# Hybrid decoder trunk, channel mixer: the value's first tap is queued ahead of SiLU, and the down projection begins with partial sums

## The reference, cut to what matters

```
def conv_gated_mlp(h, w_up, conv_w, conv_b, w_down):
    S = h.shape[1]                               # 2048
    a = h @ w_up                                 # (B, S, 2F), F = 2816
    ap = jnp.pad(a, ((0, 0), (CONV_WIDTH - 1, 0), (0, 0)))      # CONV_WIDTH = 3
    c = conv_b + sum(conv_w[j] * ap[:, j:j + S] for j in range(CONV_WIDTH))
    gate, val = jnp.split(c, 2, axis=-1)
    return (jax.nn.silu(gate) * val) @ w_down

x = x + conv_gated_mlp(rms_norm(x, norm_ffn_g[l]), w_up[l], conv_w[l], conv_b[l], w_down[l])
```

## Time and profile before

| what | value |
|---|---|
| median of 3 runs | 2349.37 us (2342.2 to 2542.82) |
| the profiled execution, own time | 2344.48 us |
| its span, slowest core (core 1) | 2343.4 us (the cores: 2335.9 to 2343.4) |
| mean granted clock of TensorE, by core | 0.934 to 0.941 |
| TensorE busy, share of the span | 2000.3 us, 85% |
| VectorE busy | 1254.0 us, 54% |
| ScalarE busy | 833.8 us, 36% |
| up projection, line 467 in all its uses | 4608 matmuls, 1097.0 us busy, 59.3 us idle before them |
| down projection, line 912 | 1408 matmuls, 311.9 us busy, 16.5 us idle before them |

### The profile page before, as it was taken

One profiled execution on the slowest core, in us unless ns is written; L12 is line 12 of the kernel. 1 busy time (PEld: TensorE's weight loads), 2 busy tenths in 40 slices (PEclk: granted clock), 3 DMA queues, 4 the chain that ended last, 5 costly groups with the idle time before them and its releaser, 6 DMA issues.

```text
span 2343.4 us, 32398 instructions; the slowest of 8 cores (2335.9 to 2343.4 us)
## 1 busy us (share of the span) xinstructions
PE 2000.3 (85%) x12288; PEld 978.8 (42%) x12288; DVE 1254.0 (54%) x1700; ACT 833.8 (36%) x1015; POOL 124.9 (5%) x240
## 2 busy tenths in 40 slices
PE   1867766899999899899996777779999899999987
PEld 1534433444444344344463434334445444444434
DVE  3534333243468748758773324333336785685776
ACT  3344444522234304224434443443223441340443
POOL 1000000000000000000010000000000000000000
PEclk9988887899999999999998878769999999999999
DMA  8101010022132222222130010102222322223213
GB/s 203 19 5 19 1 19 10 5 41 41 28 42 36 32 37 34 35 40 31 15 58 5 1 19 1 18 10 32 37 33 32 45 33 36 36 28 45 33 18 144
DMA packets 38663, 79.60 MB, mean 34 GB/s; under 512 B 4320, under 2 KB 8544, under 8 KB 38496
## 3 DMA queue, kind: packets, MB, share of 16 engines
q0 software_dynamic: 33760, 60.39, 18.2%
q1 hardware_dynamic: 4752, 17.15, 2.2%
HBM read 129.51 MB, written 8.39 MB: 59 GB/s over the span
## 4 chain that ended last, share of the span: by engine, by line
PE 71%; DVE 13%; ACT 7%; issue 6%; DMA 2%; SPq 0%; DVEq 0%; ACTq 0%
PE ps L467 38%; PE ps L912 12%; DVE tv L894 4%; PE ps L858 4%; PE ps L703 4%; ACT Pt L721 4%; PE ps L738 3%; PE ps L808 2%; PE ps L805 2%; PE ps L501 2%; ACT tv L890 2%; DMA xs<-xt 2%; DVE hs L462 1%; DVE tA L576 1%; DVE kz L488 1%
## 5 line engine op out<-in xcount | busy, mean ns | idle before, releaser
L467 PE MATMUL ps<-hs,ring 128*128 128x512 bf16 x4608 | 1097.0, 397 | 59.3 <-DVE tv L894 46.3
L467 PEld LDWEIGHTS ps<-hs,ring 128*128 128x128 bf16 x4608 | 462.8, 102 | 653.5 <-issue 170.8
L912 PE MATMUL ps<-hid,ring 128*128 128x512 bf16 x1408 | 311.9, 383 | 16.5 <-DVE hid L903 15.1
L721 ACT ACTIVATE Pt<-ps 128x1024 bf16<-128x1024 f32 x320 | 271.8, 894 | 90.4 <-PE ps L703 33.3
L894 DVE SCALAR_TENSOR_TENSOR tv<-ps,pv,tv 128x1024 f32<-128x1024 f32 (+2 forms) x176 | 225.8, 1283 | 118.9 <-ACT tv L890 109.4
L738 PE MATMUL ps<-Vt,Pt 128*128 128x65 bf16 x2176 | 132.2, 205 | 152.7 <-ACT Pt L721 146.1
L894 DVE SCALAR_TENSOR_TENSOR tg<-ps,pv,tg 128x1024 f32<-128x1024 f32 (+2 forms) x176 | 225.0, 1279 | 32.5 <-ACT tg L890 22.9
L912 PEld LDWEIGHTS ps<-hid,ring 128*128 128x128 bf16 x1408 | 138.0, 99 | 185.3 <-issue 26.6
L703 PE MATMUL ps<-qz,kz 72*128 72x512 bf16 (+3 forms) x640 | 206.2, 397 | 10.5 <-DVE qz L657 10.5
L738 PEld LDWEIGHTS ps<-Vt,Pt 128*128 128x128 bf16 x2176 | 110.6, 106 | 241.3 <-issue 224.2
L900 ACT ACTIVATE tg<-tg 128x1024 f32<-128x1024 f32 x88 | 93.1, 1058 | 317.7 <-DVE tg L894 317.6
(11 more groups left out here) (78 smaller groups left out, 1299.4 us busy)
## 6 DMA issues: line engine op xcount, KB each, us to landing
ring<-w_up POOLq DMA_DIRECT2D x88, 256.0 KB, 3.8
ring<-w_in POOLq DMA_DIRECT2D x64, 256.0 KB, 4.5
xs<-xt SPq DMA_DIRECT2D x16, 512.0 KB, 27.0
yt<-yst SPq DMA_DIRECT2D x16, 512.0 KB, 2.6
ring<-w_down POOLq DMA_DIRECT2D x32, 224.0 KB, 3.6
ring<-w_ab POOLq DMA_DIRECT2D x16, 256.0 KB, 4.6
ring<-w_out POOLq DMA_DIRECT2D x16, 256.0 KB, 4.7
ring<-w_down POOLq DMA_DIRECT2D x16, 256.0 KB, 3.8
```

Of the source, the lines that this page charges most:

```text
L467: S.op("pe", lambda e: [e.matmul(bank(b), w[:, kc, :], hs[:, c, kc, :], start=(kc == 0), stop=(kc == 7)) for kc in range(8)][-1], reads=[r ...
L721: S.op("act", lambda e: e.activation(Pt[:, pi, 0:n], ps[:, sl * 1024:sl * 1024 + n], AF.Exp, scale=0.125), reads=[PB[2 * sl], PB[2 * sl + ...
L912: S.op("pe", lambda e: [e.matmul(bank(b), w[:, kc, :], hid[:, kc, c * 512:(c + 1) * 512], start=(kc == 0), stop=(kc == nk - 1)) for kc in ...
```

## The change

In `half`, SiLU moves behind the value's first tap in ScalarE's queue. The product of the half before stays where it is. In `down`, a range of products k0 to k1 can be given. In passes 0 and 1, the first four sums are first begun with all products but the last; then each is finished, and followed by its addition. The banks' order becomes 0, 4, 1, 2, 3, 5, 6, 7. In pass 2, `accumulate` does the same for its first four sums (m = 0 to 3 of chunk 0) and takes its banks in the order 0, 4, 1, 2, 3, 5. The output projection's use of `accumulate` is unchanged.

```diff
-        def accumulate(mm, gcol, dst=None, after=None, done=None):
+        def accumulate(mm, gcol, dst=None, after=None, done=None, early=None, order=(0, 1, 2, 3, 4, 5)):
...
-                    b = nb % 6
+                    b = order[nb % len(order)]
+                    if nb == 0 and early is not None:
+                        for k in range(4):
+                            early(k, 0, order[k], 0)
+                    if nb < 4 and early is not None:
+                        early(m, c, b, 1)
+                    else:
+                        mm(m, c, b)
                     nb += 1
-                    mm(m, c, b)
...
                     if part == 0:
                         while late:
                             late.pop(0)()
-                        S.op("act", lambda e: e.activation(t, t, AF.Silu), reads=[rt[hf]], writes=[rt[hf]])
+
+                S.op("act", lambda e: e.activation(tg[:, hf, :], tg[:, hf, :], AF.Silu),
+                     reads=[R_tg[hf]], writes=[R_tg[hf]])
...
-            def down(p, m, c, b):
+            def down(p, m, c, b, k0=0, k1=None):
                 lo, hi = FPASS[p]
                 nk = hi - lo
+                k1 = nk if k1 is None else k1
                 w, rw = W(l, "dn", p, m)
                 S.op("pe", lambda e: [e.matmul(bank(b), w[:, kc, :], hid[:, kc, c * 512:(c + 1) * 512],
-                                               start=(kc == 0), stop=(kc == nk - 1)) for kc in range(nk)][-1],
-                     reads=[rw] + [R_hid[kc][c // 2] for kc in range(nk)], writes=[PB[b]])
-
-            banks = (0, 4, 5, 1, 2, 3, 6, 7)
+                                               start=(kc == 0), stop=(kc == nk - 1)) for kc in range(k0, k1)][-1],
+                     reads=[rw] + [R_hid[kc][c // 2] for kc in range(k0, k1)], writes=[PB[b]])
+
+            banks = (0, 4, 1, 2, 3, 5, 6, 7)
...
+                    early = 4
+                    for n, (m, c) in enumerate(seq[:early]):
+                        down(p, m, c, banks[n], 0, hi - lo - 1)
                     for n, (m, c) in enumerate(seq):
                         b = banks[n % 8]
-                        down(p, m, c, b)
+                        down(p, m, c, b, hi - lo - 1 if n < early else 0)
...
+            nk = FPASS[2][1] - FPASS[2][0]
+
+            def early(m, c, b, part):
+                down(2, m, c, b, 0 if part == 0 else nk - 1, nk - 1 if part == 0 else nk)
...
-                                  done=lambda m: rel(l, "dn", 2, m))
+                                  done=lambda m: rel(l, "dn", 2, m), early=early, order=(0, 4, 1, 2, 3, 5))
```

## The result

The changed kernel takes 2274.4 us, median of four runs (2271.07 to 2295.02). Against the kernel before, the ratio is 0.9691, 95% interval [0.9649, 0.9733]: 3.1% less, faster. The kernel before has a listed median of 2446.1 us in this comparison, since two of its four runs were slow (2542.82 and 2595.07 us), as runs are in which a die has a lower granted clock (one of e5's, 2542.73 us: 0.81 on four cores, 0.94 on the others) for a cause that nothing here shows, and every ratio in this document leaves such runs out. The forecast was 2269 us, 0.968 of the profiled execution; a second comparison of the same kernel, further down, gives 0.970 [0.9676, 0.9725].

The account below looks back on a forecast made before the run. TensorE was taken as the bound on average, stalled in the up projection by the VectorE, ScalarE, VectorE loop. Savings of 52.8 + 16.1 + 1.7 + 4.9 = 75.5 us took 2344.5 to 2269 us, 8-in-10 range 2260 to 2294.

Parts of the forecast that it names:

- the starting time: Whole kernel: the profiled execution's 2344.5 us taken as the time before, 4.9 us below the median of 2349.37.
- The sum: Whole kernel: 52.8 + 16.1 + 1.7 + 4.9 = 75.5 us saved, from 2344.5 to 2269.0 us.
- part 2: Ends of up projection passes: partial sums and bank order remove waits for hid, bank 5 and clock falls, 22.7 us.
- What bounds: Up projection: TensorE bounds on average, but the loop VectorE, ScalarE, VectorE takes 7.60 us a half against TensorE's 6.90.
- Part 1: Up projection: the value's first tap ahead of SiLU removes 38 TensorE stalls, 52.8 us.
- rival (B): Up projection stays at 7.6 us a half through another wait, only partial sums pay: 2321.8 us; chance 5%.
- (C): Down projection: partial sums don't pay, TensorE waits as long for the second column half: 2291.7 us; chance 11%.
- (A): Channel mixer: denser work costs TensorE its clock; 2447 us with a fifth of matmuls at the lower level; chance 4%.
- (D): Up projection: the later SiLU holds the product and by it the value taps, no gain: 2344 us; chance 2%.
- The pass of 14 halves: Up projection: a pass was to go from 108.1 to 96.6 us.
- TensorE's share: Whole kernel: TensorE's busy share of the span was to rise from 85% to 88%.
- VectorE's wait for the gate's first tap: Up projection: this wait was to rise from 22.9 to some 50 us (88 x 0.58).

Follow-up runs that it names:

- e5: Changed kernel with two more VectorE additions of 400 columns in every half; ratio 0.9878 [0.9843, 0.9913] to the kernel before, some 2320 us.
- e2: Changed kernel with SiLU back ahead of the value's first tap, leaving partial sums and bank order alone; ratio 0.9924 [0.9895, 0.9952] to the kernel before.
- e1: Kernel before with only SiLU moved behind the value's first tap, old down projection kept; ratio 0.9756 [0.9717, 0.9796] to the kernel before.
- e4: Changed kernel with one more VectorE addition of 240 columns in every half; ratio 0.9684 [0.9662, 0.9706] to the kernel before.
- e7: Changed kernel run again as it is, for a second comparison; ratio 0.9700 [0.9676, 0.9725] to the kernel before.
- e8: Changed kernel with, in each layer's first half, the last chunk's norm before the gate's taps and SiLU behind the next half's first gate tap; 0.9662 to kernel before.

## Where the prediction failed and where it held, point by point

**The step that failed: the starting time.** The sum starts from 2344.5 us and says "I take the time as it is". In the comparison the kernel before had a listed median of 2446.1 us, so that the listed medians lie 2446.1 - 2274.4 = 171.7 us apart, where the sum has 75.5. The prediction has no term for executions as long as the 2542.82 us that stood in the table of times it worked from; here they were two of four. The 96.2 us beyond the sum are not the change's: the mixers, in which all of its edits lie, are 75.4 us shorter, and the rest of the span 2.1 longer.

**The term that was mis-sized: part 2.** The prediction gave it 22.7 us. With ScalarE's order in place the partial sums bring 75.0 - 62.1 = 12.9 us; without it (e2) 16.7. The order alone brings 62.1 in place of 52.8. The mechanism of both held; the working below says which rows were put to the wrong part.

**What bounds.** Right. The up projection ran at the loop VectorE, ScalarE, VectorE. Taking only ScalarE's order away from it (e1) brings 7.60 us a half to 6.90, and giving VectorE 1.15 us more (e5) makes it the bound again.

**Part 1, 52.8 us.** Right in size and in the working. Each start that was worked out from t = 0 can be looked up, setting t = 1.57 at the gate taps of 901.40: the value's first tap was put at 3.71 and starts at 903.49 (3.66), the product at 4.16 (903.99, 4.16), the value taps at 5.30 (905.12, 5.29), the next gate taps 6.90 after the last, as measured. VectorE's gap was worked out as 0.58 and is 0.52 us. The margin of the design is therefore small but real: e4 spends 0.32 of it without loss, e5 more than all of it.

**Part 2.** The waits for hid and for bank 5 and the falls of the clock all went, 22.7 us as said; but e1 shows that ScalarE's order alone takes part of these. Its 62.1 us add up from the rows: 52.8, the six waits shrunk from 2.51 to 1.96 us (3.3), bank 5 ready in time in the old order of banks (1.7), and the falls of the clock (4.2 by the medians over the cores): 62.0. What is left for the partial sums is 6 x (1.96 + 0.17) = 12.8 us, 12.9 measured. The prediction had itself the 2 us that would remain with part 1 alone, but charged the whole 2.5, and every fall behind it, to part 2. Whether the new order of banks is needed beside the partial sums was not tried by itself. And alone (e2) they bring 16.7, not 22.7. So rival (B)'s 2321.8 us was too low; that case came out at some 2330 us. The wait that gave (C) its chance, for the second product, never occurred in the changed kernel, and occurred in e2 at the length that the same arithmetic gives.

**The sum.** 75.5 us predicted, 75.4 on the two slowest cores, 75.0 by the medians over cores. That it is so close is partly luck: layer 1's mixer stood at 471.3 us, not 470.0, on one of the eight cores, and in e7 on six. The whole time came out 2 to 5 us above 2269: 2271.07 in the profiled run and 2274.4 in the median. The working took the time of one execution; the medians of this kernel lie a few us above it, before and after.

**The rivals.** (A) did not come. The window 696 to 1096 us, from layer 0's first half to its last up projection, on cores 0 and 1 (all eight have 1.00):

```profile
696.00:1096.00 400.00, 394.18 (x1793) 178.97 (x1829) 307.36 (x282) 142.27 (x128) 30.61 (x58) 1.00 0.26 37
696.00:1096.00 400.00, 400.00 (x1853) 181.15 (x1851) 306.91 (x278) 143.78 (x129) 31.67 (x60) 1.00 0.27 38
```

TensorE is busy for 394 to 400 of 400 us on all cores (the 394 where records are missing), at full clock. The rule of the Trainium skill ("TensorE: Matmul & The Clock Gate", Part 1), 13/16 of the clock for sustained dense matmuls on all cores, does not describe this execution. (B) and (D) are refuted by e1, (C) by the waits after.

**What the profile was to show.** The pass of 14 halves: 96.6 predicted, 951.57 - 854.88 = 96.69. TensorE's share: 88%, as said. VectorE's wait for the gate's first tap: some 50 predicted, 62.6 measured. Here a term was left out: 22.9 us of such waits at the starts of the passes were there before and stay; 80 x 0.52 + 22.9 = 64.5.

## What to carry to other kernels

In a queue that is worked in order, an instruction whose input is late must not stand ahead of one whose input is there and for which another engine waits; move the late one back until its own reader would notice, and count that reader's slack. Compare the period of the loop between the helpers with the period of the main engine by itself: the difference, times the turns that stall, is the gain. Here that is 15.19 - 13.80 = 1.39 us for two halves, 38 times, 52.8 us; the drain behind each stall (0.17) is already in it. Do this sum for one edit at a time: the whole held to 1%, while one part came out 18% larger and the other 43% smaller. Where a stage ends in a product that the next needs last, begin a few of the next stage's sums without it, for a little longer than the wait; here more of them bought nothing.

## What the runs showed that was not expected

A fall of the clock is not tied to one length of wait. On the core shown of the kernel before it came behind three of six waits of 2.5 us. Over its eight cores it came behind all 16 such waits at the end of pass 0 and behind 5 of the 32 at the ends of passes 1 and 2, though all are 2.5 us long; this makes up most of the 1.6 us by which layer 1's mixer scatters there. With waits of 2.0 us (e1) it came behind 2 of 48, at the same price of 1.7 us. Behind the waits of 1.2 us in the up projection of the core shown it came in none: their runs of 64 are 13.97 us long, but for one of 14.13 with a granted clock of 1.00.

The price differs too. Behind the 3.88 us wait in layer 1, the run of 472 is 103.57 us on core 5 of the changed kernel's execution and 104.87 on core 7, and in e7 104.87 on core 3; this is the 1.3 us by which layer 1's mixer stands at 470.0 or 471.3 us. Over the first 5.6 us of such a run the granted clock is 0.72 on core 1 (103.57) and 0.50 on core 7. What decides which waits are hit, and how hard, was not tried.

The second finding is about measuring. One profiled execution gives the mixer on eight cores to within 0.5 us in layer 0 (1.9 in e1, where the clock fell on one core), while whole times of one kernel scatter by 5 to 10 us, since the attention stretches do. A gain of 1 us in a stage (e8) is plain in the stage and invisible in the median.
